# Byte positions of the matrix operands in SBUF: rows of split inputs 1024 bytes apart, weight slots from multiples of 512

## What is computed

```
def rmsnorm(x, g):  y = x * rsqrt(mean(x * x) + 1e-6);  return y * g
def swiglu(h, w13, w2):  g, u = split(h @ w13, 2);  return (silu(g) * u) @ w2
for i in range(4):                        # mixers: conv, attention, hyena, conv
    x = x + mixer_i(rmsnorm(x, mix_g[i])) # h @ w_in (1024 x 3072), mixing, y @ w_out (1024 x 1024)
    x = x + swiglu(rmsnorm(x, ffn_g[i]), w13[i], w2[i])   # hidden width 2816
# second network: proj = u @ w_in (1024 x 5792); retention and latent attention on its parts;
# merged = sigmoid(g1) * (ret @ w_ret_out) + sigmoid(g2) * (lat @ w_mla_out); x + merged @ w_o; swiglu
```

## Time and profile before

| | us |
|---|---|
| median of 3 runs | 1797.13 |
| lowest and highest | 1794.29 and 1799.27 |
| span of the profiled execution | 1795.4 |
| TensorE busy in it | 1740.3 (97%) |
| VectorE busy | 1228.8 (68%) |
| ScalarE busy | 974.9 (54%) |
| DMA, mean over the span | 162 GB/s |

### The profile page before, as it was taken

One profiled execution on the slowest core, in us unless ns is written; L12 is line 12 of the kernel. 1 busy time (PEld: TensorE's weight loads), 2 busy tenths in 40 slices (PEclk: granted clock), 3 DMA queues, 4 the chain that ended last, 5 costly groups with the idle time before them and its releaser, 6 DMA issues.

```text
span 1795.4 us, 37239 instructions
## 1 busy us (share of the span) xinstructions
PE 1740.3 (97%) x13776; PEld 1647.1 (92%) x13776; DVE 1228.8 (68%) x2013; ACT 974.9 (54%) x1352; POOL 12.8 (1%) x20
## 2 busy tenths in 40 slices
PE   7999999998999999999999999999999999999997
PEld 7999999998999988569999999999999877799997
DVE  6886666587766587888666588666566665576654
ACT  4467744365775454207774446775454644467742
POOL 0000200000000000000000000000000000000000
PEclk9999999999999999999999999999999999999999
DMA  6567564533766554105566456657454431256661
GB/s 208 166 202 223 187 223 132 160 107 97 245 192 209 165 165 140 60 1 177 186 195 204 149 169 181 199 181 241 152 176 141 137 133 60 72 175 187 187 215 66
DMA packets 79545, 290.15 MB, mean 162 GB/s; under 512 B 9739, under 2 KB 12140, under 8 KB 79340
## 3 DMA queue, kind: packets, MB, share of 16 engines
q1 hardware_dynamic: 79468, 289.11, 51.3%
HBM read 288.03 MB, written 1.05 MB: 161 GB/s over the span
## 4 chain that ended last, share of the span: by engine, by line
PE 86%; DVE 9%; ACT 2%; issue 2%; DVEq 0%; DMA 0%; SPq 0%; ACTq 0%
PE bank L521 25%; PE bank L523 24%; PE bank L522 24%; DVE wlo L1464 2%; PE bank L809 2%; PE bank L796 1%; PE bank L750 1%; DVE rinv L1470 1%; PE bank L905 1%; PE bank L1001 1%; DVE conv_cv L1572 1%; ACT whi L1098 1%; PE bank L974 1%; PE bank L1011 1%; PE bank L730 1%
## 5 line engine op out<-in xcount | busy, mean ns | idle before, releaser
L521 PE MATMUL bank<-xh,whi 128*128 128x256 f32 (+1 forms) x2736 | 776.2, 284 | 7.5 <-DVE wlo L1464 7.3
L522 PE MATMUL bank<-xl,whi 128*128 128x256 f32 (+1 forms) x2736 | 771.2, 282 | 0.0
L523 PE MATMUL bank<-xh,wlo 128*128 128x256 f32 (+1 forms) x2736 | 770.6, 282 | 0.0
L1098 ACT CAST whi<-raw 128x1024 fp32r<-128x1024 f32 (+1 forms) x490 | 538.4, 1100 | 363.5 <-PE bank L523 324.1
L1464 DVE TENSOR_TENSOR wlo<-raw,whi 128x1024 fp32r<-128x1024 f32 (+1 forms) x491 | 629.6, 1282 | 4.8 <-ACT whi L1098 2.7
L521 PEld LDWEIGHTS bank<-xh,whi 128*128 128x128 f32 x2736 | 517.5, 189 | 24.0 <-DVE wlo L1464 12.4
L523 PEld LDWEIGHTS bank<-xh,wlo 128*128 128x128 f32 x2736 | 518.3, 189 | 0.0
L522 PEld LDWEIGHTS bank<-xl,whi 128*128 128x128 f32 x2736 | 514.7, 188 | 1.3 <-issue 1.2
L521 PE MATMUL bank<-ffn_hh,whi 128*128 128x256 f32 x880 | 246.7, 280 | 0.0
L523 PE MATMUL bank<-ffn_hh,wlo 128*128 128x256 f32 x880 | 246.7, 280 | 0.0
L522 PE MATMUL bank<-ffn_hl,whi 128*128 128x256 f32 x880 | 245.8, 279 | 0.0
(11 more groups left out here) (322 smaller groups left out, 2028.5 us busy)
## 6 DMA issues: line engine op xcount, KB each, us to landing
raw<-in_w SPq DMA_DIRECT2D x414, 512.0 KB, 3.6
raw<-in_w SPq DMA_DIRECT2D x80, 704.0 KB, 4.2
att_bias<-in_bias SPq DMA_DIRECT2D x4, 512.0 KB, 5.5
hy_w<-in_filt_w SPq DMA_DIRECT2D x8, 256.0 KB, 5.2
hy_decay<-in_decay SPq DMA_DIRECT2D x4, 512.0 KB, 4.4
mla_uq<-in_uq SPq DMA_DIRECT2D x1, 1152.0 KB, 5.3
x<-in_xT SPq DMA_DIRECT2D x1, 1024.0 KB, 5.8
out<-x SPq DMA_DIRECT2D x8, 128.0 KB, 2.0
```

The source lines that it names most:

```text
L521: pe.matmul(ps, whi[:, slot, wc], hi[:, k, cols], start=first, stop=False)
L522: pe.matmul(ps, whi[:, slot, wc], lo[:, k, cols], start=False, stop=False)
L523: mm = pe.matmul(ps, wlo[:, slot, wc], hi[:, k, cols], start=False, stop=last)
L1098: nc.scalar.copy(whi[:, p % RING, 0:k * P], raw[:, p % RING, 0:k * P]).then_inc(panel_hi, 1)
```

## The change

Nothing is computed otherwise, and no wait is added or taken away. It moves data in SBUF.

* 384 bytes are put ahead of `raw`. `raw`, `whi`, `wlo` then start at multiples of 512, and as a slot is 11 x 512 and a block 512 bytes, every block of weights does too.
* `xq["h"]` and `xq["l"]` overlay `xh` and `xl`. They have 8 rows of 256 floats, 1024 bytes apart, and the space saved lies behind them as a gap. All products of 256 columns read them in place of `xh[:, k, A]` and `xl[:, k, A]`. Products of 272 columns still read `xh` and `xl`, whose rows stay 1088 bytes apart, now from a multiple of 256.
* 192 more bytes are put behind PSUM's declaration, ahead of the overlays. `ffn["hh"]`, `ffn["hl"]`, `yh`, `yl` and the others get rows of 1024 bytes with a gap behind each tensor. In the built program all of them start at a multiple of 256, but `ffn["hl"]`, which starts 128 bytes past one: its neighbour `hh` with its gap is 22 x 1088 bytes long.
* The other overlay tensors behind them move by 576 bytes.

```
+    sb("align_weights", [P, 96])
+    def rows(name, n):
+        return [(name, [P, n, SEQ], F32R), (name + "_gap", [P, n * META], F32)]
...
+    xq = overlay("xq", rows("h", C) + rows("l", C))
     xh = sb("xh", [P, C, L], F32R)
...
+    sb("align_rows", [P, 48])
...
-    ffn = overlay("ffn", [("hh", [P, FC, L], F32R), ("hl", [P, FC, L], F32R)])
-    Y = [("yh", [P, C, L], F32R), ("yl", [P, C, L], F32R)]
+    ffn = overlay("ffn", rows("hh", FC) + rows("hl", FC))
+    Y = rows("yh", C) + rows("yl", C)
...
+    def split_of(cols):
+        return (xq["h"], xq["l"], Q) if cols == A else (xh, xl, B)
...
-            product(f"up{layer}", xh, xl, A, (x_lo, C * norm), norm)
+            product(f"up{layer}", xq["h"], xq["l"], Q, (x_lo, C * norm), norm)
             norm += 1
-            product(f"down{layer}", ffn["hh"], ffn["hl"], A, (hid_lo, FC * layer))
+            product(f"down{layer}", ffn["hh"], ffn["hl"], Q, (hid_lo, FC * layer))
...
-            V.scalar_tensor_tensor(out=xl[:, m, cols], in0=x[:, m, cols], scalar=gain,
-                                   in1=xh[:, m, cols].bitcast(F32), op0=ALU.mult,
+            hi, lo, split_cols = split_of(cols)
+            V.scalar_tensor_tensor(out=lo[:, m, split_cols], in0=x[:, m, cols], scalar=gain,
+                                   in1=hi[:, m, split_cols].bitcast(F32), op0=ALU.mult,
```

More of the change, by code:

```diff
@@ L681, in out_slices @@
                         wc = slice(k * P, (k + 1) * P)
-                        pe.matmul(ps, whi[:, slot, wc], at["yh"][:, k, A], start=k == 0, stop=False)
-                        pe.matmul(ps, whi[:, slot, wc], at["yl"][:, k, A], start=False, stop=False)
-                        mm = pe.matmul(ps, wlo[:, slot, wc], at["yh"][:, k, A], start=False, stop=k == C - 1)
+                        pe.matmul(ps, whi[:, slot, wc], at["yh"][:, k, Q], start=k == 0, stop=False)
+                        pe.matmul(ps, whi[:, slot, wc], at["yl"][:, k, Q], start=False, stop=False)
+                        mm = pe.matmul(ps, wlo[:, slot, wc], at["yh"][:, k, Q], start=False, stop=k == C - 1)
                         if k == C - 1:
                             mm.then_inc(panel_used, 1)
-            first_panels(ph, xh, xl, A, (x_lo, C * norm), norm, A)
+            first_panels(ph, xq["h"], xq["l"], Q, (x_lo, C * norm), norm, A)
             pe.wait_ge(na["loaded"], 16)
             for m in range(2, 16):
-                panel(ph, 0, m, xh, xl, A, None)
+                panel(ph, 0, m, xq["h"], xq["l"], Q, None)
                 if m >= 2:
@@ L713, in attention @@
             for j in range(2, 8):
-                panel(PH["out1"], j // 4, j % 4, at["yh"], at["yl"], A, None)
+                panel(PH["out1"], j // 4, j % 4, at["yh"], at["yl"], Q, None)
         def hyena(norm):
@@ L778, in out_slices @@
                         wc = slice(k * P, (k + 1) * P)
-                        pe.matmul(ps, whi[:, slot, wc], hy["yh"][:, k, A], start=k == 0, stop=False)
-                        pe.matmul(ps, whi[:, slot, wc], hy["yl"][:, k, A], start=False, stop=False)
-                        mm = pe.matmul(ps, wlo[:, slot, wc], hy["yh"][:, k, A], start=False, stop=k == C - 1)
+                        pe.matmul(ps, whi[:, slot, wc], hy["yh"][:, k, Q], start=k == 0, stop=False)
+                        pe.matmul(ps, whi[:, slot, wc], hy["yl"][:, k, Q], start=False, stop=False)
+                        mm = pe.matmul(ps, wlo[:, slot, wc], hy["yh"][:, k, Q], start=False, stop=k == C - 1)
                         if k == C - 1:
@@ L813, in hyena @@
             for p in range(4, 24):
-                panel(ph, p // 4, p % 4, xh, xl, A, None)
+                panel(ph, p // 4, p % 4, xq["h"], xq["l"], Q, None)
                 if p in (4, 13):
@@ L846, in hyena @@
             for j in range(3, 8):
-                panel(PH["out2"], j // 4, j % 4, hy["yh"], hy["yl"], A, None)
+                panel(PH["out2"], j // 4, j % 4, hy["yh"], hy["yl"], Q, None)
         def retention_in(norm):
@@ L1036, in _ @@
             else:
-                product(f"in{layer}", xh, xl, A, (x_lo, C * norm), norm)
+                product(f"in{layer}", xq["h"], xq["l"], Q, (x_lo, C * norm), norm)
             if layer == 0:
@@ L1050, in _ @@
         latent()
-        product("mla_out", ml["yh"], ml["yl"], A, None)
-        product("w_o", mg["yh2"], mg["yl2"], A, (y_lo, YBASE["mrg"]))
-        product("up4", xh, xl, A, (x_lo, C * norm), norm)
+        product("mla_out", ml["yh"], ml["yl"], Q, None)
+        product("w_o", mg["yh2"], mg["yl2"], Q, (y_lo, YBASE["mrg"]))
+        product("up4", xq["h"], xq["l"], Q, (x_lo, C * norm), norm)
         norm += 1
-        product("down4", ffn["hh"], ffn["hl"], A, (hid_lo, FC * DEPTH))
+        product("down4", ffn["hh"], ffn["hl"], Q, (hid_lo, FC * DEPTH))
         total(norm, A)
```

45 lines of the change are left out of this document (23 added, 22 removed).

## The result

The changed kernel takes 1810.0 us (median of 4 runs, 1806.2 to 1812.6), the kernel before 1796.0 in the runs beside it (4 runs, 1794.3 to 1799.3). The ratio is 1.0078, with a 95% interval of 1.0059 to 1.0098: slower, by 14 us. The forecast was 1750, faster. It had the wrong direction; the time lies within the wide range of 1722 to 1816 only because that range reached up to the second rival.

What follows compares the result with a forecast made beforehand. The prediction took TensorE's interval per product as the bound. 42.8 us from unbroken stretches and 4.2 us from products between DVE and ACT work made 47 us, span 1748.4, median 1750, range 1722 to 1816.

Steps and rivals of the forecast that it cites:

- the second rival: Aligned position is bad: distance 0 between weights and input settles at 120 ns a product, 1817 us; chance 0.27.
- The bound: Whole kernel: TensorE's own pace counts, busy 1740 of 1795 us, so the interval of one product sets the time.
- All rows at one offset, weights at one offset: Split products of 256 columns: 12,216 moved, settling at 114 ns instead of 118.2, together 47 us saved.
- row k = 6: Input row in the first two panels, 64 bytes past a multiple of 256; its products settled at 113 ns.
- Row k = 7: Input row in the first two panels, 128 bytes past a multiple of 256; five intervals of 118 ns each.
- One row in four already starts at a multiple of 256: Reason given against the gain at 114 ns: the stretch as a whole shows no gain by such rows.
- 272 columns at 0 change: 360 products in in_ret and in_mla: rows and weights both move 128 bytes, distance stays, 126.2 ns kept; 0 us.
- The register instruction in `x_low`: DVE work in 8 residuals: between 0 and 27 us of DVE time, mostly hidden; taken as 0.
- DVE, ACT and DMA at new positions: Their reads and writes move too; nothing in the rows shows they depend on position; taken as 0.
- The rate of supply: In up0, whether DVE, ACT and DMA keep up at 114 ns; DMA busy 0.69, nothing else comes due.
- Positions only shuffle the loss: Rival for the split products: loss per product is fixed and moves between neighbours, no change, 1797 us; chance 0.19.
- The page's rule: Trainium skill: TensorE's weight and moving ports are independent, SBUF lines 16 bytes, so nothing would change; sum 0.

Runs made afterwards that it cites:

- weights_alone: The kernel before with 384 bytes of padding ahead of the weight slots, every distance between rows and weights kept; 1795.2 us, ratio 1.000.
- w64_r0: The changed kernel with weights 64 bytes past a multiple of 256 and input rows at multiples, distance 192; 1770.4 us, ratio 0.9863 to the kernel before.
- both experiments on position: weights_alone, and the changed kernel with weights and input rows both moved by 64 bytes, distance still 0, at 1810.2 us, ratio 1.0076.
- w64_r0_hl: w64_r0 with 128 bytes more behind `hh`, so that `ffn["hl"]` has distance 192 too; 1766.3 us, ratio 0.9857 to the kernel before.
- w0_r192_hl: The changed kernel with weights at multiples of 256 and all inputs, `hl` too, moved to 192 past one; 1765.9 us, ratio 0.9858.
- the half load: The changed kernel with the second of three products loading 64 weight columns instead of 128, also writing only 64 partitions; 1779.6 us in one run.

## Why the prediction was wrong

*The bound* was right. TensorE's interval sets the time, the waits of others did not come up, and the experiments moved the span by about what their intervals say.

*The failing step* is "All rows at one offset, weights at one offset". It put 114 ns, 4.2 under the kernel before, where the changed kernel took 120.0, 1.7 over it. It took the value of row k = 6, and the row was read rightly: 113 ns is real, and it is the interval of the short rhythm. But I took it as the value of a good position in general, and gave fewer crossings of 256-byte pieces as the reason. weights_alone has fewer crossings of the weights and gains nothing; w64_r0, whose blocks of weights touch three pieces as before, gains 26 us. Row k = 6 starts 64 bytes past a multiple of 256 and the weights 128 past, so its distance is 192. Row k = 7 has distance 0, the one that the change makes, and its last interval rose to 120. The prediction worked out the distance for k = 7 in the second rival, and not for k = 6. With both worked out, k = 6 says nothing of the change, and k = 7 puts it at 118 to 120, not at 114. "One row in four already starts at a multiple of 256" was no argument either way, since position does not count.

A second error is in the count. 744 of the 12,216 products were not moved to a new distance at all, though the section on the change says that all products of 256 columns read `xq`. At the forecast's 4.2 ns these are 3 us.

*The second rival* is what happened, mechanism and stretch: "419 or fewer" was named, and 419 came. It had a chance of 0.27. Its 120 ns were read from the last intervals of a single row, but that was no accident of this row, as the end of this section shows. Its time, 1817, was 7 too high. It counted 1.8 ns on 11,208 products. `down` with its `hl` at 128 did not take part, 2,640 x 1.8 = 4.8 us, nor did the 744 products in rows of 1088 bytes, 1.3 us: 1811.

*Other terms.* 272 columns at 0 change: right, and so was the reason. Their start times average 126.0 ns in `in_ret` of the kernel before, of the changed one and of both experiments on position. `ffn["hl"]` was to make `down` either 114 or nothing; it was nothing, 117.9 to 117.8. That `hl` decides was shown at 192, where moving it brought 113.3. The register instruction in `x_low`: 0, DVE's total is the same. DVE, ACT and DMA at new positions: 0, right. The rate of supply: nothing else came due, even in w64_r0_hl, where the counts in 50 us are 4% above those of the kernel before.

*Positions only shuffle the loss*: wrong as a mechanism. With one distance throughout, the interval goes from 113.3 ns to 120.0; it is not fixed. But neither is it a sum of what each distance takes alone: where the four distances rotate it is 118.2 on average, and the mean of the four values found above is 117.5.

*The page's rule.* Distances of 0 and 192 are 40 us apart here, in kernels that differ in padding alone. The Trainium skill, "SBUF — State Buffer", section "Who interferes with whom", has TensorE's port for weights independent of that for the moving operand, by which they would be alike. The measurement decides: for these float32r products with a load of 128 x 128 weights each, where the two operands lie to each other sets the pace.

The profile before held what was needed, but only in one place. In the steady stream of the five `up`, three products on a row, the start times sorted by the row's distance give 117.5 ns for 64, 118.6 for 128, 119.0 for 192 and 118.1 for 0: the later best comes last, so a row's neighbours count there as much as the row. The first two panels tell more, as six products follow on one row. Over all ten stages that begin so, the last two intervals of a row average 117.8 ns at distance 64, 118.6 at 128, 113.4 at 192 and 119.2 at 0, where the very last is 121. These are nearly the values of the kernels with one distance throughout. What had to be read is where a run on one row ends up, and for every distance.

## What to carry to other kernels

Where each product loads its own weights and the interval is above both the stream and the load, work out (start of the input row - start of the weights) modulo 256 for all of them, and test a few constant distances by padding alone. Here 192 was the best and 0, the one that "aligned" gives, the worst. Take several runs of each, as one execution at 64 or 192 can have more or fewer stretches at 113.3 ns than the next. A row stride that is a multiple of 256 only fixes the distance, it does not make it good; check that all operands take part, and do not take an absolute alignment for the aim. w64_r0_hl and w0_r192_hl are the versions to keep, 1.4% faster than the kernel before.

## What the runs showed that I had not expected

* The intervals are not noise around a mean but exact rhythms. At 2.4 GHz (granted clock 1.00 in these stretches) 113.33 ns are 272 cycles, 16 more than the columns; 120.0 ns are 288, 32 more; with the half load 350 ns for three are 3 x 280.
* At distance 192 there are two rhythms, 113.3 and 117.8 ns, and at 64 the same two, with the long one far more often. The state outlives a thousand products and the passage from `up` to `down`. In three profiled executions at 192 (two of w64_r0_hl, one of w0_r192_hl) none of 216 unbroken stretches changes its rhythm; it changes only where the stream breaks, as for 1.06 us in the rows above. The length of the break bears on it: where the next split product started 221 to 223 ns after the last one, 72 of 79 stretches were short, and after 226 ns all 12 were long. But breaks of different lengths stand in different places of the program, so what decides is not shown. A way to force the short rhythm wasn't tried. By the profiled execution of 1756.5 us, in which `up1` and `down1` had the long one, it would give a span of about 1756.5 - 4.5 - 2.3 = 1750, an estimate.
* The good distance is narrow: 32 bytes off 192 on either side lose 26 us again, 1792 for both. 160 has two values of its own, 117.3 and 118.7 ns by the start times.
